# Tiles turned by transposing DMAs instead of TensorE, with the engines' order set anew, in a windowed-attention and gMLP layer

## The reference, cut to what matters

```
h      = modulate(layer_norm(x), shift, scale)                 # per channel
q,k,v,u,vb,ga,gb = split(h @ w_in)
ya     = window_attention(rope(q), rope(k), v, kc, vc, sink)   # +-128 tokens, plus 256 context keys
yb     = gelu(u) * (W_s LN(gelu(vb)) + b)                      # per chunk of 128 tokens
mix    = (sigmoid(ga) * (ya @ w_a) + sigmoid(gb) * (yb @ w_b)) @ w_out
x_mid  = layer_norm(alpha * x + gate * mix)
h2     = modulate(layer_norm(x_mid), shift2, scale2)
x_new  = layer_norm(alpha * x_mid + gate2 * ((silu(h2 @ wg) * (h2 @ wu)) @ w_out2))
```

## Time and profile before

| | us |
|---|---|
| median of 3 runs | 956.84 |
| lowest, highest run | 956.53, 1048.83 |
| the profiled execution's own time | 957.48 |
| its span on the slowest core (core 4) | 955.9 |
| spans of the 8 cores | 947.8 to 955.9 |
| TensorE (PE) busy | 888.3 (93%) |
| VectorE (DVE) busy | 620.6 (65%) |
| ScalarE (ACT) busy | 303.3 (32%) |
| GpSimd (POOL) busy | 307.4 (32%) |

### The profile page before, as it was taken

One profiled execution on the slowest core, in us unless ns is written; L12 is line 12 of the kernel. 1 busy time (PEld: TensorE's weight loads), 2 busy tenths in 40 slices (PEclk: granted clock), 3 DMA queues, 4 the chain that ended last, 5 costly groups with the idle time before them and its releaser, 6 DMA issues.

```text
span 955.9 us, 15754 instructions; the slowest of 8 cores (947.8 to 955.9 us)
## 1 busy us (share of the span) xinstructions
PE 888.3 (93%) x5509; PEld 444.1 (46%) x5605; DVE 620.6 (65%) x1126; ACT 303.3 (32%) x477; POOL 307.4 (32%) x235
## 2 busy tenths in 40 slices
PE   0498899999999999999999999999999999999995
PEld 0344545444554444444444444444444444444673
DVE  4437797766555677766685575656556574676787
ACT  0433766647677144433435101011110101111110
POOL 6027586347553243334321720220202021111111
PEclk9999899999999999999999999999999999999998
DMA  8996740199763400036403560312303020111112
GB/s 199 196 200 192 155 121 25 43 168 169 130 103 76 177 1 1 1 114 108 132 1 133 125 184 1 89 26 63 88 1 89 1 44 1 44 45 67 45 67 89
DMA packets 30382, 83.93 MB, mean 88 GB/s; under 512 B 2912, under 2 KB 3168, under 8 KB 28640
## 3 DMA queue, kind: packets, MB, share of 16 engines
q0 software_dynamic: 18064, 34.54, 22.9%
q1 hardware_dynamic: 12240, 48.37, 14.4%
HBM read 109.05 MB, written 8.39 MB: 123 GB/s over the span
## 4 chain that ended last, share of the span: by engine, by line
PE 84%; DMA 8%; DVE 3%; issue 2%; POOL 2%; ACT 0%; SPq 0%; DVEq 0%; POOLq 0%; ACTq 0%
PE psum L1198 31%; PE psum L1224 15%; PE psum L1036 11%; PE psum L1087 6%; PE psum L1053 6%; DMA arena<-wu 5%; PE psum L916 3%; PE psum L678 2%; DMA arena<-xh 2%; PE psum L956 2%; PE psum L765 2%; DMA arena<-wout 1%; DVE arena L496 1%; PE psum L734 1%; PE psum L468 1%
## 5 line engine op out<-in xcount | busy, mean ns | idle before, releaser
L1198 PE MATMUL psum<-arena 128*128 128x512 bf16 (+1 forms) x1513 | 314.4, 361 | 1.2
L1198 PEld LDWEIGHTS psum<-arena 128*128 128x128 bf16 x1536 | 150.2, 98 | 154.5
L1204 ACT ACTIVATE arena<-psum 128x512 f32<-128x512 f32 (+1 forms) x96 | 53.8, 561 | 373.5 <-PE psum L1198 373.5
L1224 PE MATMUL psum<-arena 128*128 128x512 bf16 x682 | 160.9, 379 | 1.8 <-DVE arena L1207 0.7
L1238 DVE TENSOR_TENSOR arena<-arena,psum 128x512 f32<-128x512 f32 x224 | 140.6, 681 | 18.5 <-PE psum L1224 18.5
L509 POOL TENSOR_TENSOR arena<-arena 128x1 f32<-128x1 f32 (+1 forms) x74 | 74.4, 1005 | 238.0 <-DVE arena L507 230.4
L1207 DVE TENSOR_TENSOR arena<-psum,arena 128x512 bf16<-128x512 f32 (+1 forms) x96 | 62.1, 647 | 131.0 <-PE psum L1198 128.1
L1036 PE MATMUL psum<-arena 128*128 128x512 bf16 x491 | 114.9, 379 | 2.5 <-issue 1.1
L496 DVE BATCH_NORM_STATS2 arena<-arena 128x6 f32<-128x512 f32 x152 | 99.7, 685 | 16.7 <-DMA arena<-xh 10.5
L1224 PEld LDWEIGHTS psum<-arena 128*128 128x128 bf16 x704 | 68.6, 98 | 82.7 <-issue 2.6
L925 ACT ACTIVATE arena<-psum 128x1024 bf16<-128x1024 f32 (+1 forms) x100 | 80.8, 853 | 22.3 <-PE psum L916 17.1
(11 more groups left out here) (102 smaller groups left out, 927.3 us busy)
## 6 DMA issues: line engine op xcount, KB each, us to landing
arena<-xh SPq DMA_DIRECT2D x34, 512.0 KB, 7.8
arena<-wada POOLq DMA_DIRECT2D x24, 512.0 KB, 9.0
arena<-wff POOLq DMA_DIRECT2D x11, 1024.0 KB, 9.2
arena<-wff SPq DMA_DIRECT2D x11, 1024.0 KB, 6.5
out<-arena SPq DMA_DIRECT2D x15, 512.0 KB, 2.6
arena<-wc POOLq DMA_DIRECT2D x8, 768.0 KB, 15.3
arena<-wout SPq DMA_DIRECT2D x8, 512.0 KB, 4.7
arena<-rope SPq DMA_DIRECT2D x4, 512.0 KB, 8.1
```

Source lines behind the costliest of these rows:

```text
L1198: ins = e.matmul(bank(ps)[:, 0:n], lhsT=w1v[r][:, k, lo:lo + 128], rhs=h2(k), start=(k == 0), stop=(k == 7))
L1204: s = P.op('act', prio - 150, act_cost(n), lambda e: e.activation(out=sgv(), in_=bank(pg)[:, 0:n], func=AF.Silu), after=[a], takes=[sg], g ...
L1224: ins = e.matmul(bank(ps), lhsT=actv[(r, fi, t)], rhs=w2v[r][:, fi, h * 512:(h + 1) * 512], start=(n == 0), stop=(n == 2 * len(rounds) - 1))
```

## The change

It does this:

- Groups 1, 2, 3 and hal are turned by one transposing DMA per tile (128x1024 bf16, 256 KB, 16 of them), issued by SP from `xnb` straight into `hT` (`hal`, `hcT`). The modulation then works in place, from SBUF to SBUF, 8 calls per group. Group 0 still uses TensorE.
- Each tile's attention result is turned by one transposing DMA (128x512 bf16, 128 KB, 16 of them) from `yatm` over its q. The four TensorE transposes and VectorE's copy go.
- Each second norm is turned by one transposing DMA (256 KB, 16 of them) from `xb` into `hT`; the modulation works in place.
- Which engine normalises: group 2 is on VectorE and ScalarE (VectorE and POOL before), group 3 on ScalarE and VectorE (VectorE and POOL), hal on ScalarE alone (VectorE and ScalarE). `ZPOOL = 0` moves the scaling of L784 to ScalarE. Modulation is shared between ScalarE and VectorE: 3, 6, 3 of 8 calls on VectorE in groups 1, 2, 3 (none before), and 4 of 8 for each half of hal (as before).
- The second gate vector `g2bc` lies over `bsbc` and `wst` and is formed at priority 480 (595 before). `act_free` is kept by group of tiles. The load of ln2 waits for the transposing DMAs too and stands apart from the lane's order.
- The priorities of most operations before the FFN change, among them those of the w_out multiplication (48.2 + 2k, 126.8 + 2k before).

```
@@ norm_group
-        for c2 in range(4):
-            def put(ps, tr, c2=c2):
...
-            turn(['%s_%d' % (name, i) for i in range(4)], prio + 0.5, c2, put)
+        tds = []
+        for i in range(4):
+            n, xb, turned_by = xn_of['%s_%d' % (name, i)]
+            if name != 'hal':
+                dst = lambda i=i: hT[:, :, int(name) * 512 + i * 128: int(name) * 512 + (i + 1) * 128]
+            else:
+                dst = lambda i=i: (hal if i < 2 else hcT)[:, :, i % 2 * 128:(i % 2 + 1) * 128]
+            td = P.dma('sp', prio + -13.1, 256, lambda e, xb=xb, dst=dst: e.dma_start_transpose(
+                out=dst(), in_=V(o_xnb[sid(xb)], BF16, 1024)), lambda xb=xb: 'xnb%d' % sid(xb), after=[n], gives=[xb])
...
+                t_h[(g, c)] = P.op(eng, prio + 2.6, cost, lambda e, c=c, eng=eng, g=g: modulate_out(
+                    e, eng, hT[:, c, g * 512:(g + 1) * 512], hT[:, c, g * 512:(g + 1) * 512], 1, 0, c, 0),
+                    after=tds + need)
@@
+    HALEV = alternate(4)
+    HEV = {1: alternate(3), 2: alternate(6), 3: alternate(3)}
-    norm_group('2', ..., 47.5, [ld_wu[1]], ('dve', 'pool'))
-    norm_group('hal', ..., 20.1, [ld_wu[3]], ('dve', 'act'))
+    norm_group('2', ..., 80.0, [ld_wu[1]], ('dve', 'act'))
+    norm_group('hal', ..., 62.3, [ld_wu[3]], ('act', 'act'))
-    ZPOOL = 1
+    ZPOOL = 0
-    ld_x3 = norm_group('3', ..., 90.5, [ld_wu[1]], ('dve', 'pool'), room=(7, 8, 0, 1, 2, 3))
+    ld_x3 = norm_group('3', ..., 99.5, [ld_wu[1]], ('act', 'dve'), room=(7, 8, 0, 1, 2, 3))
-        t_wo.append(P.op('dve', 126.8 + 2 * k, 1.5, ...
+        t_wo.append(P.op('dve', 48.2 + 2 * k, 1.5, ...
-    proj_v(1, 60.5)          -    proj_u(1, 90.7)     -    proj_qk(2, 90.9)    -    proj_u(2, 100.3)
+    proj_v(1, 50.9)          +    proj_u(1, 79.7)     +    proj_qk(2, 76.7)    +    proj_u(2, 102.3)
...
@@ attend
-        tb = banks(*X)
...
-        tr = P.op('pe', prio + 0.7, 0.28, ft, after=norms, takes=[tb], gives=[ytm])
-        t_ya[j] = P.op('dve', prio + 0.7, 0.42, lambda e: e.tensor_copy(
-            out=qv[:, :, jt * 128:(jt + 1) * 128], in_=bankb(tb)[:, 0:512].rearrange('p (a b) -> p a b', a=4)),
-            after=[tr, q_last], gives=[tb])
+        t_ya[j] = P.dma('sp', prio + -7.4, 128, lambda e: e.dma_start_transpose(
+            out=qv[:, :, jt * 128:(jt + 1) * 128], in_=V(L['yatm'] + KB * sid(ytm), BF16, 512)), lambda: 'ya%d' % sid(ytm),
+            after=norms + [q_last], gives=[ytm])
@@ residual
-            tiles.append((n, xb, xbv))
+            td = P.dma('sp', prio + i, 256, lambda e, xbv=xbv, t=t: e.dma_start_transpose(
+                out=hT[:, :, t * 128:(t + 1) * 128], in_=xbv()), lambda xb=xb: 'xb%d' % sid(xb),
+                after=[n] + [h_done[(m_, g)] for m_ in range(8)], gives=[xb])
...
-                tr = P.op('pe', prio + i, 0.5, f, after=[p[0] for p in pair], takes=[ps], gives=[p[1] for p in pair])
...
+            for c in range(8):
+                t_h2[(g, i // 2, c)] = P.op('act', prio + i, ..., modulate_out(
+                    e, 'act', hT[:, c, cut], hT[:, c, cut], 4, 3, c, 0),
+                    after=tiles[-2:] + [modc_ready[(3, c)], modc_ready[(4, c)]])
@@ FFN
-    g2bc = V(o_xn, F32, 1024)
+    g2bc = V(L['bsbc'], F32, 1024)
-        act_free[r % 2] = [m for t in range(NT) for m in dn_mm[(r, t)]]
+        act_free[r % 2] = [[m for t in range(4 * g, 4 * g + 4) for m in dn_mm[(r, t)]] for g in range(NTG)]
```

More of the change, by code:

```diff
@@ L585, in build_nc @@
     t_hal, t_hc = {}, {}
+    tr_last = []
+    alternate = lambda n: ['dve' if (c + 1) * n // 8 > c * n // 8 else 'act' for c in range(8)]
+    HALEV = alternate(4)
+    HEV = {1: alternate(3), 2: alternate(6), 3: alternate(3)}
     for i in (0, 2):
@@ new lines, in norm_group @@
+        for c in range(8):
+            need = [modc_ready[(kd, c)] for kd in (0, 1)]
+            if name == 'hal':
+                eng = HALEV[c]
+                cost = 0.58 if eng == 'act' else 0.3
+                t_hal[c] = P.op(eng, prio + -28.8, cost, lambda e, c=c, eng=eng: modulate_out(
+                    e, eng, hal[:, c, :], hal[:, c, :], 1, 0, c, 0), after=tds[:2] + need)
+                t_hc[c] = P.op(eng, prio + -8.7, cost, lambda e, c=c, eng=eng: modulate_out(
+                    e, eng, hcT[:, c, :], hcT[:, c, :], 1, 0, c, 1), after=tds[2:] + need)
+            else:
+                g = int(name)
+                eng = HEV[g][c]
+                cost = 0.82 if eng == 'act' else 0.55
+                t_h[(g, c)] = P.op(eng, prio + 2.6, cost, lambda e, c=c, eng=eng, g=g: modulate_out(
+                    e, eng, hT[:, c, g * 512:(g + 1) * 512], hT[:, c, g * 512:(g + 1) * 512], 1, 0, c, 0),
+                    after=tds + need)
@@ L1160, in build_nc @@
     wo_all = [wo_done[(t, h)] for t in range(NT) for h in range(2)]
-    act_free = [[wo_done[(t, h)] for t in ts for h in range(2)] for ts in (range(8, 12), range(12, 16))]
-    g2bc = V(o_xn, F32, 1024)
-    xb_free = [t_h2[(3, x, c)] for x in range(2) for c in range(8)]
-    t_g2 = [spread(5, h, 595, DU, g2bc, xb_free) for h in range(2)]
-    ld_ln2 = load('sp', 640, 1024, V(o_m, F32, 2048), ln2_d, 'ln2', after=[t_xm[t] for t in range(NT)])
+    act_free = [[[wo_done[(t, h)] for t in ts for h in range(2)]] * NTG for ts in (range(8, 12), range(12, 16))]
+    g2bc = V(L['bsbc'], F32, 1024)
+    gmlp_done = list(t_yb.values()) if isinstance(t_yb, dict) else list(t_yb)
+    t_g2 = [spread(5, h, 480, DU, g2bc, gmlp_done) for h in range(2)]
+    ld_ln2 = load('sp', 640, 1024, V(o_m, F32, 2048), ln2_d, 'ln2', after=[t_xm[t] for t in range(NT)] + tr_last, apart=True)
     w1s = [slot('w1', i) for i in range(0)]
@@ L1199, in f @@
             return ins
-        a = P.op('pe', prio, 1.73 * nt / 4, lambda e: f(e, pg, fi * 128), after=need + [ld_w1[r]], takes=[pg])
+        a = P.op('pe', prio, 1.73 * nt / 4, lambda e: f(e, pg, fi * 128), after=need + [ld_w1[r]], behind=after, takes=[pg])
         b = P.op('pe', prio, 1.73 * nt / 4, lambda e: f(e, pu, 256 + fi * 128), after=need + [ld_w1[r]], behind=[a], takes=[pu])
```

101 lines of the change are left out of this document (44 added, 57 removed).

## The result

The median of 4 runs is 998.32 us (996.20 to 999.77). The kernel before gave 956.76 beside it. The ratio is 1.043, with a 95% interval of 1.0417 to 1.0443. The prediction said 935 us with a range to 951, and no more than 2% slower with a chance of 0.92. It was wrong in sign and by 63 us.

What follows compares the result with a forecast made beforehand. It took the kernel as DMA-bound to 50 us, mixed with stalls to about 220, TensorE-bound after. Transposes, stalls, group 1's DMAs and SP gave 957.5 - 17.4 - 8.1 + 3 + 1 = 936.0, stated as 935 us, range 922 to 951.

Steps and rivals of the forecast that it cites:

- What the 48 DMAs cost: Price of the transposing DMAs: 0.75 us per 256 KB tile, so +3 us for group 1's four before 50.09 us.
- SP is strict as well: SP's list: x, rope and w_out loads stand behind waiting DMAs; +1 us, for residual x loads after the attention.
- Groups 2, 3 and hal: Norm groups: transposes leaving TensorE save 1.8 us for group 3 and 4.8 for groups 2 and hal.
- two times about 25 us: Projections of groups 0 and 1 from 50 us on, said to cover the DMA latency of groups 2, 3 and hal.
- if it went, each group would cost 2 to 4 us: Cost of groups 2, 3 and hal should the cover by projections of groups 0 and 1 fail.
- about 2 us: DMA latency, with a place behind loads, replacing 1.7 us or more of TensorE in groups 2, 3 and hal.
- The stalls, -8.1 us: TensorE's early waits and slow clock, 80 to 220 us: -3.1 - 0.8 - 2.7 - 1.5 us gained.
- w_out, of which I took 1.5: At 200 to 220 us: earlier w_out multiplication frees buffers and spreads w_ada loads; 1.5 us gained, bounds 0 and 3.
- second norms: On the dense TensorE path: 128 transposes at 0.056 us removed, 7.1 us gained.
- attention: Nearly all on the dense TensorE path: 64 transposes at 0.057 us removed, 3.7 us gained.
- D: Rival: transposing DMAs slow and one after another, delaying group 1, groups 2 and hal, and attention; 980 to 1010 us, chance 0.10.
- C: Rival: early lists give the stalls back, SP holds loads, 5 to 10 us of new waits; 942 to 957 us, chance 0.24.

Runs made afterwards that it cites:

- e6: The kernel before with attention results and second norms turned by transposing DMA, priorities and engines unchanged: 945.81 us, ratio 0.9862.
- e13: e6 with group 1 alone turned by transposing DMA too: 972.89 us, ratio 1.0172.
- e18: The kernel before with all 48 turned tiles by transposing DMA, its priorities and engines kept: 990.96 us, ratio 1.0356.
- e8: The changed kernel with every transpose back on TensorE: 983.10 us, ratio 1.024.
- e1: The changed kernel with group 1 alone turned by TensorE again, lists planned anew: 978.10 us, ratio 1.0184.
- e3: As e2, and group 0's rope table issued ahead of group 1's transposing DMAs: 982.16 us, ratio 1.0236.
- e2: The changed kernel with group 1's modulations placed behind group 0's q and k on VectorE's and ScalarE's lists: 992.73 us, ratio 1.0346.
- e9: e6 with groups 2, 3 and hal turned by transposing DMA too, group 1 still on TensorE: 968.90 us, ratio 1.009.
- e12: e6 with group 3 alone turned by transposing DMA too: 953.04 us, ratio 0.9944.
- e17: e12 with the second and later w_c loads waiting for the last w_out load to land: one time, 941.97 us.
- e4: The kernel before with only the second norms turned by transposing DMA: 951.29 us, ratio 0.9922.
- e5: The kernel before with only the attention results turned by transposing DMA: 953.87 us, ratio 0.9946.
- e7: The changed kernel with POOL's loads cut into pieces of at most 2048 B (4096 before): one time, 991.78 us.

## Why the prediction was wrong

The account, by differences of ratios, is a path: e6 -13.2; group 1 added (e13 - e6) +29.7; groups 2, 3 and hal added (e18 - e13) +17.6; the new order added (changed kernel - e18) +7.0. Together +41.1 us. Along another path the items have other sizes: the new order alone +23.0 (e8), all DMAs but group 1's -5.4 (e1 - e8), group 1's +23.5, together +41.1. So the costs partly cover each other.

- **The failed step: "What the 48 DMAs cost", group 1.** I had both ends, 0.6 and 11.5 us a tile, and took 0.75 because a store of the same bytes was the nearest row. That row comes from the end of the kernel, where POOL's queue is idle. Group 1's tiles run where the earlier trace rows show one weight piece of 43.81 us in flight. There the far end was right in number: 44.4 us for four tiles, against 46 worked out and 3 taken. It was right by luck. It gave every 256 B the mean packet time of queue 1 itself (0.18 us), while a piece takes some 0.026 us and waits for a packet of the other queue, which happens to be as long (0.173 us). Nor are the 44.4 us the loss: most of the 23.5 to 29.7 us came by the waits of the next point, as e3 is only 5.0 us above e1.
- **"SP is strict as well"** named x, rope and w_out loads, and costed only the one after the attention. At the start, the loads of rope and of the attention sink behind the DMAs are a hold of 23.9 us by themselves (e2). Nor did I read the new lists of VectorE and ScalarE there: eight modulations that used to wait for TensorE now wait for DMAs, ahead of what the first projection needs.
- **Groups 2, 3 and hal**, taken as -6.6 with the cover "two times about 25 us": measured +17.6 to +21.8. The sentence "if it went, each group would cost 2 to 4 us" was too small as well. The step that failed is the latency of "about 2 us" behind a cover: in the changed kernel the eight tiles of groups 2 and hal land 4.8 to 11.3 us after issue, and the wait for the last stands on the chain before 143.08 us. In e9 it is the same wait (5.79 us at 111.26) and the slow clock after it; the rest of the 17.6 to 21.8 us isn't traced. In e12 most of group 3's 7.8 us is the collision of w_out with w_c (e17), which neither e9 nor the changed kernel has.
- **The stalls, -8.1 us:** wrong in sign. The new order costs 23.0 us by itself (e8), through the engine choice (6.4) and the priorities (9.9) and some 7 that neither carries alone; which wait the 6.4 and the 9.9 are isn't shown. For w_out, of which I took 1.5, the earlier priority didn't bring the last load forward: in the changed kernel it leaves at 245.7 us in place of 199.0.
- **Right:** second norms -7.1 predicted and -7.5 measured (e4), attention -3.7 and -5.2 (e5; the 1.5 more isn't explained), each transpose priced by the start of the next row. Together (e6) they give 13.2 us.
- **The rivals.** The time lies in D's span of 980 to 1010, and for group 1 D had the price and the consequence: it had the group through at 82 us (73.2). Its reason, that transposing DMAs are slow in themselves, is wrong, and so is its second half: groups 2 and hal were through at 142.1 us and not 174, and attention's first scores came 31 us late (150.2 after 119.1) and not 60. That the total fell into D's span is thus partly luck. C had the kind of waits right (loads held on SP, new holes) and their size (5 to 10 us) much too small. I gave D 0.10 since I judged its price by one unloaded row.

## What to carry to other kernels

Price a DMA by what else is in the queues at its place, not by a row from a quiet stretch: many small pieces beside long packets of another queue take one such packet's time each. Before a step moves from a compute engine to a queue, list what is behind it on that queue and on the engines that read it. And when an order is set anew, measure the order without the change and the change without the order: here two of the six uses (attention and second norms) gave 13 us in the old order, and no run shows a gain from any other.

## What the runs showed beyond what was expected

- A transposing DMA of 256 KB holds SP's sequencer for 1.2 us where POOL's queue is idle and for up to 12.1 us beside the weight loads (13.3 in e3).
- Smaller packets in one queue speed up the other (e7, one run): 0.173 to 0.103 us a packet, and 29.7 to 20.9 us for the four tiles.
- One 512 KB load landed 15.4 us after issue beside three loads of 768 KB and about 6.8 beside one (e12, e17), and some 9 us of the whole went with it.
